# Query and key projections of a hybrid attention block: one wide matmul for the high and low activations, with the PSUM banks of attention moved

## The chip, the cores and the metric

The kernel runs on one core of one Trainium2 chip. The metric is the device time of one execution, in microseconds. Only that one core works; no other core's clock or traffic plays a part. TensorE (matmuls into PSUM), VectorE, ScalarE, GpSimd and the DMA queues each run their own stream of instructions and meet at semaphores.

## What is computed

One layer of an encoder block on 256 tokens of width 2048, all in float32, then a final normalisation. Cut to what matters here:

```python
h = rms_norm(x, norm_mix)
proj = h @ w_in                       # 2048 -> qa 1024, ka 256, va 256, qf 1024, kf 1024, vf 1024, f 16
qa, ka = rope(qa), rope(ka)           # group A: 16 query heads, 4 key heads, head width 64
out_a = swa_sink_attention(qa, ka, va, sinks)          # sliding window of two 64-token chunks
log_f = log_sigmoid(f_logit + b_f)
out_b = forgetting_attention(qf, kf, vf, log_f)        # group B ("FoX"): 16 heads, causal, no rotary
x = x + concat([out_a, out_b]) @ w_o
h = rms_norm(x, norm_ffn)
x = x + conv_gated_ffn(h, w_up, conv_w, conv_b, w_down)   # d_ff 5632
return rms_norm(x, norm_final)
```

## The kernel before

**Float32 products from split parts.** Every operand of a projection is split into a high part that TensorE's replicated float32 type (R32) holds exactly, and a low part, the rest. ScalarE makes the high part (`split_hi`, L417: `hi` from `raw`), VectorE the low part (`split_lo`, L645: `lo` = `raw` - `hi`). A product is then high times high, high times low and low times high: `mm3` (L960 to L964), three matmuls. The activations are held turned, features on partitions, in `act_split[:, 2, 16, 256]`: the high parts of the 16 blocks of 128 features (`act_hi`) beside their low parts (`act_lo`).

**Tiles of weights.** The weights stream through four slots (`RING`). A tile is 512 KB: 512 rows by 256 columns for `w_in` and `w_up`. Tiles are numbered through the kernel: 0 to 3 hold the values of group A and the gates, 4 to 7 the keys of group A, 8 + 16 j + s is step s of quad j (j from 0 to 3), from 72 on come W_o, the up and the down projection. For tile t SyncE loads `raw` when `lo_done` shows tile t - 4 split, ScalarE splits when `mm_done` shows tile t - 4 multiplied, then VectorE, then TensorE multiplies (`pe.wait_ge(lo_done, t + 1)`). Both splitters run three tiles ahead (`LEAD`): at step s of a quad they split the tile of step s + 3.

**Quads.** A quad is four query heads of each group and takes 16 tiles, four each for qa, kf, qf (function `features`, weights stationary, the result features by tokens) and vf (function `tokens`, activations stationary). In `features` a pair (c, b) is one block of 128 input features by one block of 128 output features: three matmuls of 256 columns. The results of qa and qf went to bank `acc[0]`, kf, vf and the keys of group A to `acc[1]`: both blocks b of one result share one bank of 512 columns.

**Out of PSUM.** VectorE scales kf (step 8) and qf (step 12) out of PSUM in one instruction each (L773), and makes the rotary embedding: `rope` (L675, from PSUM times cosine, step 5) and `rope_rest` (L680, L682, step 9), where `swap` is a copy with the halves of each head exchanged, made by ScalarE's `rope_swap` (L435, step 4) out of PSUM in four instructions.

**Attention** of quad j - 1 runs beside the projections of quad j. The steps are constants: scores behind step 13, the maxima and biases at 14 (VectorE reads the FoX scores at L735, ScalarE takes exponentials), then in the next quad the turned copies through `tr_ps` at steps 1 to 3 (ScalarE L506, L510), the products with the values behind step 4 (L1070 `values_a` into `pv_ps`, L1081 `values_fox` into `acc[2]`), and their evacuation at 5 (ScalarE L514, VectorE L765).

**Around the keys of group A** (tiles 4 to 7), ScalarE's stream is: high part of tile 10, `rope_swap`, `fcum`, wait for `krope_s`, four copies to `kta` (L484), high part of tile 11 and on. VectorE's: low part of tile 10, rope in three instructions, low part of tile 11 and on. GpSimd waits for `kta`, copies group A's operands, writes `nft` to memory, reads it back as `key_bias` four times 512 KB, and adds the causal mask to it in eight instructions (L394, L395), in quad 0.

**The up projection** (`up_step`, L1206 to L1213) multiplies otherwise: one matmul of the high weights with `act_split[:, :, k, :]`, 512 columns, high and low activations side by side in one bank, and one of the low weights with the high activations, 256 columns, onto the first half. ScalarE and VectorE add the two halves of the bank when they take it out.

## Time and profile before

| what | value |
|---|---|
| median of 3 runs | 1089.55 us (1089.06 to 1089.94) |
| the profiled execution's own time | 1088.71 us |
| its span, first to last instruction | 1086.8 us |
| TensorE busy | 1075.6 us, 99% of the span |
| VectorE / ScalarE / GpSimd busy | 710.2 / 579.6 / 27.4 us |
| HBM read and written | 199.06 and 2.11 MB |

The profile is of one execution. Engine names in its rows: PE is TensorE (PEld its weight loads), DVE is VectorE, ACT ScalarE, POOL GpSimd, SP SyncE; a q behind a name is that engine's sequencer. Matmuls overlap in the pipeline, so a matmul's listed duration is longer than its share of TensorE's time. Idle time stands in brackets in a timeline row with what ended it. The time lies 1.9 us over the span, for what comes before the first and after the last instruction.

### The profile page before, as it was taken

Reading aid. Unit: us, or ns where it says so; the run is one execution under the profiler, and the core shown is the slowest. Engines: PE = TensorE matmul, PEld = TensorE weight load, DVE = VectorE, ACT = ScalarE, POOL = GpSimd, SP = SyncE. Lnnn points to the kernel's source line nnn. Section 1 sums busy time; section 2 is a strip of 40 time slices with the busy share of each in tenths; the row PEclk is TensorE's granted clock in tenths of the full one; section 3 lists DMA queues with packets and bytes.
Section 4 is the critical chain, followed back from the end, with each engine's and each line's share of the span. In section 5 each row is a group of like instructions: output and inputs, shape, how many; then the busy total and the mean of one; then the engine's idle time right before and its main releaser. Section 6 shows DMA issues by size and latency. Waiting matters only on the chain.

```text
span 1086.8 us, 18571 instructions
## 1 busy us (share of the span) xinstructions
PE 1075.6 (99%) x6553; PEld 947.1 (87%) x6553; DVE 710.2 (65%) x1023; ACT 579.6 (53%) x890; POOL 27.4 (3%) x42
## 2 busy tenths in 40 slices
PE   8999999999999999999999999999999999999997
PEld 8999999998888888888888888888888888888885
DVE  5667575656555787777777777877777444454543
ACT  6847373736455655565555555566555434343432
POOL 1150000000000000000000000000000000000000
PEclk9999999999999999999999999999999999999999
DMA  9685645454555666656665566656666656656662
GB/s 275 192 268 152 174 138 174 143 179 142 174 174 176 179 202 191 183 172 208 190 196 177 180 206 192 183 169 209 193 192 212 206 187 190 192 184 189 191 190 101
DMA packets 169796, 201.69 MB, mean 186 GB/s; under 512 B 8580, under 2 KB 136292, under 8 KB 169632
## 3 DMA queue, kind: packets, MB, share of 16 engines
q1 hardware_dynamic: 168464, 197.49, 58.9%
q0 software_dynamic: 976, 3.37, 1.0%
q8 instruction: 24, 0.39, 0.1%
q10 hardware_dynamic: 320, 0.34, 0.1%
q14 instruction: 12, 0.10, 0.0%
HBM read 199.06 MB, written 2.11 MB: 185 GB/s over the span
## 4 chain that ended last, share of the span: by engine, by line
PE 98%; DMA 1%; SPq 0%; DVE 0%; ACT 0%; issue 0%; DVEq 0%
PE tr_ps L1210 15%; PE acc L1210 15%; PE acc L962 8%; PE acc L963 8%; PE acc L964 8%; PE acc L1212 8%; PE tr_ps L1212 8%; PE sc_ps L962 5%; PE sc_ps L963 5%; PE sc_ps L964 5%; PE tr_ps L963 4%; PE tr_ps L962 4%; PE tr_ps L964 4%; DMA nat<-x 1%; PE tr_ps L1098 0%; PE acc L1081 0%
## 5 line engine op out<-in xcount | busy, mean ns | idle before, releaser
L645 DVE TENSOR_TENSOR lo<-raw,hi 128x1024 fp32r<-128x1024 f32 (+1 forms) x368 | 448.5, 1230 | 285.7 <-ACT hi L417 285.4
L417 ACT ACTIVATE hi<-raw 128x1024 fp32r<-128x1024 f32 (+1 forms) x368 | 384.6, 1058 | 262.1 <-PE sc_ps L964 78.9
L1210 PE MATMUL tr_ps<-act_split,hi 128*128 128x512 f32 x704 | 245.3, 391 | 0.0
L1210 PE MATMUL acc<-act_split,hi 128*128 128x512 f32 x704 | 245.0, 391 | 0.0
L1212 PE MATMUL acc<-act_split,lo 128*128 128x256 f32 x704 | 197.1, 280 | 0.0
L1212 PE MATMUL tr_ps<-act_split,lo 128*128 128x256 f32 x704 | 197.1, 280 | 0.0
L1210 PEld LDWEIGHTS acc<-act_split,hi 128*128 128x128 f32 x704 | 131.6, 187 | 28.9
L1210 PEld LDWEIGHTS tr_ps<-act_split,hi 128*128 128x128 f32 x704 | 131.7, 187 | 28.8
L1212 PEld LDWEIGHTS tr_ps<-act_split,lo 128*128 128x128 f32 x704 | 133.0, 189 | 0.1
L1212 PEld LDWEIGHTS acc<-act_split,lo 128*128 128x128 f32 x704 | 133.1, 189 | 0.0
L962 PE MATMUL acc<-act_split,hi 128*128 128x256 f32 x416 | 118.9, 286 | 0.0
L964 PE MATMUL acc<-act_split,lo 128*128 128x256 f32 x416 | 117.7, 283 | 0.0
L963 PE MATMUL acc<-act_split,hi 128*128 128x256 f32 x416 | 117.7, 283 | 0.0
L962 PEld LDWEIGHTS acc<-act_split,hi 128*128 128x128 f32 x416 | 79.7, 192 | 0.5 <-issue 0.5
L963 PEld LDWEIGHTS acc<-act_split,hi 128*128 128x128 f32 x416 | 79.8, 192 | 0.0
L964 PEld LDWEIGHTS acc<-act_split,lo 128*128 128x128 f32 x416 | 79.7, 192 | 0.0
L964 PE MATMUL sc_ps<-hi,g_lo 128*128 128x512 f32 x176 | 69.4, 395 | 0.0
L963 PE MATMUL tr_ps<-lo,g_hi 128*128 128x512 f32 x176 | 69.4, 395 | 0.0
L962 PE MATMUL tr_ps<-hi,g_hi 128*128 128x512 f32 x176 | 69.4, 395 | 0.0
L962 PE MATMUL sc_ps<-hi,g_hi 128*128 128x512 f32 x176 | 69.4, 394 | 0.0
L963 PE MATMUL sc_ps<-lo,g_hi 128*128 128x512 f32 x176 | 69.4, 394 | 0.0
L964 PE MATMUL tr_ps<-hi,g_lo 128*128 128x512 f32 x176 | 69.4, 394 | 0.0
(207 smaller groups left out, 1292.3 us busy)
## 6 DMA issues: line engine op xcount, KB each, us to landing
raw<-w_up SPq DMA_DIRECT2D x176, 512.0 KB, 4.4
raw<-w_down SPq DMA_DIRECT2D x88, 512.0 KB, 4.5
raw<-w_in SPq DMA_DIRECT2D x72, 512.0 KB, 3.7
raw<-w_o SPq DMA_DIRECT2D x32, 512.0 KB, 3.8
nat<-x SPq DMA_DIRECT2D x8, 256.0 KB, 6.3
key_bias<-nft_dram POOLq DMA_DIRECT2D x4, 512.0 KB, 8.3
result<-nat SPq DMA_DIRECT2D x7, 256.0 KB, 3.0
gfin<-norm_final POOLq DMA_DIRECT2D x1, 1024.0 KB, 7.9
```

The source lines that it names most:

```text
L417: act.activation(hi[:, slot, 0:n], raw[:, slot, 0:n], ACT.Copy).then_inc(hi_done, 1)
L645: dve.tensor_tensor(lo[:, slot, 0:n], raw[:, slot, 0:n], hi[:, slot, 0:n].bitcast(F32), ALU.subtract).then_inc(lo_done, 1)
L962: pe.matmul(dst, a_hi, b_hi, start=start, stop=False, skip_group_check=True)
L963: pe.matmul(dst, a_hi, b_lo, start=False, stop=False, skip_group_check=True)
L964: return pe.matmul(dst, a_lo, b_hi, start=False, stop=True, skip_group_check=True)
L1210: pe.matmul(up_banks[v][b].rearrange("p (a n) -> p a n", a=2), wh[:, c, b * P:(b + 1) * P], act_split[:, :, k, :], start=k == 0, stop=Fals ...
L1212: ins = pe.matmul(up_banks[v][b][:, 0:S], wl[:, c, b * P:(b + 1) * P], act_hi[:, k], start=False, stop=True, skip_group_check=True)
```

## The change

`features` takes up the form of the up projection: for each pair (c, b) one matmul of the high weights with high and low activations side by side (512 columns) and one of the low weights with the high activations (256 columns). One result now fills two banks, so the five banks `acc[0..2]`, `pv_ps` become one tensor `pj` of four: qa and qf in banks 0 and 1 (pair 0), the keys of group A and kf in 2 and 3 (pair 1), vf in 2. The products with the values and the cumulated gates go to `tr_ps`, the second pair of FoX scores to `pj[:, 3]` and `pj[:, 0]`.

To add the halves, ScalarE copies the second half of both banks into the result's place in SBUF (`cross_half`), and VectorE adds the first half from PSUM (`join_halves`); then kf and qf are scaled in place, and rope runs on `rope_a` in SBUF. `rope_swap` now reads `rope_a`, so it waits for `join_halves`: at step 6 in a quad (was 4), and VectorE's three rope instructions stand together at step 7 (were at 5 and 9). TensorE's waits: the first tile of a quad also waits for `read_s` (VectorE has read the previous quad's FoX scores), `values_a` for all three turned copies, and the scores for `kq_s` (kf and qf scaled). The diff's core:

```diff
-QUAD_STEPS = 7
+QUAD_STEPS = 8
...
-        acc = [ps(f"acc{i}", [P, 512]) for i in range(3)]
+        pj = ps("pj", [P, 4, 512])
         sc_ps = ps("sc_ps", [P, 2, 512])
         tr_ps = ps("tr_ps", [P, 2, 512])
-        pv_ps = ps("pv_ps", [P, 512])
-        x_banks = [acc[0][:], acc[2][:], acc[1][:], sc_ps[:, 0], sc_ps[:, 1], tr_ps[:, 0], tr_ps[:, 1], pv_ps[:]]
-
-        wo_banks = [(sc_ps[:, 0], sc_ps[:, 1]), (acc[0][:], acc[1][:])]
-        yt_banks = (acc[2][:], pv_ps[:])
-
-
-        fox_banks = [(tr_ps[:, 0], tr_ps[:, 1]), (acc[2][:], pv_ps[:])]
-
-        up_banks = [[tr_ps[:, 0], tr_ps[:, 1]], [acc[1][:], acc[2][:]]]
+        x_banks = [pj[:, 0], pj[:, 1], pj[:, 2], sc_ps[:, 0], sc_ps[:, 1], tr_ps[:, 0], tr_ps[:, 1], pj[:, 3]]
+
+        wo_banks = [(sc_ps[:, 0], sc_ps[:, 1]), (pj[:, 1], pj[:, 2])]
+        yt_banks = (pj[:, 3], pj[:, 0])
+
+
+        fox_banks = [(tr_ps[:, 0], tr_ps[:, 1]), (pj[:, 3], pj[:, 0])]
+
+        up_banks = [[tr_ps[:, 0], tr_ps[:, 1]], [pj[:, 0], pj[:, 1]]]
...
-            def rope_swap(bank, scale):
-
+            def rope_swap(scale):
+
+                part = rope_a[:].rearrange("p a n -> p (a n)")
                 for o in range(0, P, 32):
                     i = o ^ 32
-                    ins = act.activation(swap[o:o + 32].rearrange("p a n -> p (a n)"), bank[i:i + 32, :], ACT.Copy, scale=scale)
+                    ins = act.activation(swap[o:o + 32].rearrange("p a n -> p (a n)"), part[i:i + 32], ACT.Copy, scale=scale)
                 ins.then_inc(swap_s, 1)
+
+            def cross_half(pair, dst):
+
+                act.activation(dst[:], pj[:, 2 * pair:2 * pair + 2, S:2 * S], ACT.Copy).then_inc(half_s, 1)
...
                 if s == 3:
                     act.wait_ge(mm_done, T_KA + 4)
-                    rope_swap(acc[1], 1.0)
+                    cross_half(1, rope_a)
                     act.wait_ge(fcum_ps, 1)
-                    act.activation(fcum[:].rearrange("p a n -> p (a n)"), pv_ps[:, 0:MT * NH], ACT.Copy,
+                    act.activation(fcum[:].rearrange("p a n -> p (a n)"), tr_ps[:, 0, 0:MT * NH], ACT.Copy,
                                    scale=-1.0).then_inc(fcum_s, 1)
+                    act.wait_ge(evac_d, 1)
+                    rope_swap(1.0)
                     act.wait_ge(krope_s, 1)
...
                 for s in range(QUAD_TILES):
+                    if s in (8, 12):
+                        act.wait_ge(mm_done, j * QUAD_TILES + (T_QUAD + s))
+                        if attend:
+                            act.wait_ge(sf_s, j * 2)
+                        if s == 8:
+                            cross_half(1, kf)
+                        else:
+                            cross_half(0, qf)
                     split_hi(j * QUAD_TILES + (T_QUAD + s + LEAD), (s + LEAD) % RING)
                     if s == 4:
                         act.wait_ge(mm_done, j * QUAD_TILES + (T_QUAD + 4))
                         act.wait_ge(krope_s, j + 1)
-                        rope_swap(acc[0], QSCALE)
+                        cross_half(0, rope_a)
+                    if s == 6:
+                        act.wait_ge(evac_d, j * 3 + 2)
+                        rope_swap(QSCALE)
...
-            def rope(bank, scale, tmp):
-
-                dve.scalar_tensor_tensor(tmp[:], bank[:].rearrange("p (a n) -> p a n", a=2), scale,
-                                         cos_r[:].unsqueeze(1).broadcast_to([P, 2, S]), ALU.mult, ALU.mult).then_inc(evac_d, 1)
-
-            def rope_rest(dst, tmp):
-
+            def join_halves(pair, dst, n):
+
+                dve.wait_ge(half_s, n)
+                dve.tensor_tensor(dst[:], dst[:], pj[:, 2 * pair:2 * pair + 2, 0:S], ALU.add).then_inc(evac_d, 1)
+                dve.wait_ge(evac_d, n)
+
+            def rope(dst, scale):
+
+                st.done(dve.scalar_tensor_tensor(rope_a[:], rope_a[:], scale,
+                                                 cos_r[:].unsqueeze(1).broadcast_to([P, 2, S]), ALU.mult, ALU.mult))
                 st.done(dve.tensor_tensor(swap[:], swap[:], sin_r[:].unsqueeze(1).broadcast_to([P, 2, S]), ALU.mult))
                 st.wait()
-                return dve.tensor_tensor(dst[:], tmp[:], swap[:], ALU.add)
+                return dve.tensor_tensor(dst[:], rope_a[:], swap[:], ALU.add)
...
-                    dve.wait_ge(mm_done, T_KA + 4)
+                    join_halves(1, rope_a, 1)
                     dve.wait_ge(swap_s, 1)
-                    rope(acc[1], 1.0, rope_a)
-                    dve.wait_ge(evac_d, 1)
-                    rope_rest(rope_b, rope_a).then_inc(krope_s, 1)
+                    rope(rope_b, 1.0).then_inc(krope_s, 1)
...
                 for s in range(QUAD_TILES):
                     if s in (8, 12):
-                        dve.wait_ge(mm_done, j * QUAD_TILES + (T_QUAD + s))
-                        bank, dst, scale = (acc[1], kf, 1.0) if s == 8 else (acc[0], qf, QSCALE)
-                        dve.scalar_tensor_tensor(dst[:], bank[:].rearrange("p (a n) -> p a n", a=2), scale,
-                                                 r1b[:].unsqueeze(1).broadcast_to([P, 2, S]), ALU.mult,
-                                                 ALU.mult).then_inc(evac_d, 1)
+                        pair, dst, scale = (1, kf, 1.0) if s == 8 else (0, qf, QSCALE)
+                        join_halves(pair, dst, j * 3 + (3 if s == 8 else 4))
+                        dve.scalar_tensor_tensor(dst[:], dst[:], scale, r1b[:].unsqueeze(1).broadcast_to([P, 2, S]), ALU.mult,
+                                                 ALU.mult).then_inc(kq_s, 1)
                     split_lo(j * QUAD_TILES + (T_QUAD + s + LEAD), (s + LEAD) % RING)
-                    if s == 5:
-                        dve.wait_ge(mm_done, j * QUAD_TILES + (T_QUAD + 4))
+                    if s == 4:
+                        join_halves(0, rope_a, j * 3 + 2)
+                    if s == 7:
                         dve.wait_ge(swap_s, j + 2)
-                        rope(acc[0], QSCALE, rope_a)
-                    if s == 9:
-                        dve.wait_ge(evac_d, j * 3 + 2)
-                        rope_rest(qa, rope_a).then_inc(krope_s, 1)
+                        rope(qa, QSCALE).then_inc(krope_s, 1)
...
-            def features(t, slot, bank, kt, a_hi, a_lo, first):
+            def features(t, slot, pair, kt, first):
 
                 pe.wait_ge(lo_done, t + 1)
                 wh, wl = narrow(hi, slot), narrow(lo, slot)
                 for c in range(4):
+                    k = 4 * kt + c
                     for b in range(2):
-                        ins = mm3(bank[:, b * S:(b + 1) * S], wh[:, c, b * P:(b + 1) * P], wl[:, c, b * P:(b + 1) * P],
-                                  a_hi[:, 4 * kt + c], a_lo[:, 4 * kt + c], start=first and c == 0 and b == 0)
+                        bank = pj[:, 2 * pair + b]
+                        pe.matmul(bank.rearrange("p (a n) -> p a n", a=2), wh[:, c, b * P:(b + 1) * P], act_split[:, :, k, :],
+                                  start=first and c == 0, stop=False, skip_group_check=True)
+                        ins = pe.matmul(bank[:, 0:S], wl[:, c, b * P:(b + 1) * P], act_hi[:, k], start=False, stop=True,
+                                        skip_group_check=True)
                 ins.then_inc(mm_done, 1)
...
                 pe.wait_ge(evac_d, j * 3 + 4)
+                pe.wait_ge(kq_s, j * 2 + 2)
...
-                pe.wait_ge(pt_s, q * 3 + 1)
+                pe.wait_ge(pt_s, q * 3 + 3)
                 for v, c0, c1, moving in ((0, 0, 2, lambda h: turned_a[:, h, :, :, 0:64]),
                                           (1, 2, 3, lambda h: turned_a[:, h, 1:2, :, 64:128]),
                                           (2, 3, 4, lambda h: turned_a[:, h, 0:1, :, 64:128])):
                     for h in range(2):
-                        dst = pv_ps[h * HD:(h + 1) * HD].rearrange("k (e c n) -> k c e n", e=2, c=4)[:, c0:c1]
+                        dst = tr_ps[h * HD:(h + 1) * HD, 0].rearrange("k (e c n) -> k c e n", e=2, c=4)[:, c0:c1]
                         ins = pe.matmul(dst, vq[:, v], moving(h), start=v == 0, stop=True, skip_group_check=True)
...
             def values_fox(q):
 
-                pe.wait_ge(pt_s, q * 3 + 3)
                 pe.wait_ge(evac_a, q + 2)
                 for p in range(2):
                     for k in range(2):
                         for h in range(2):
                             i = p * 2 + h
-                            ins = pe.matmul(acc[2][h * HD:(h + 1) * HD, p * S + k * P:(p + 1) * S], vf[:, k, i * HD:(i + 1) * HD],
+                            ins = pe.matmul(tr_ps[h * HD:(h + 1) * HD, 1, p * S + k * P:(p + 1) * S], vf[:, k, i * HD:(i + 1) * HD],
...
                                 pe.wait_ge(evac_d, j * 3 + 1)
+                                pe.wait_ge(read_s, j * 2)
                             else:
                                 pe.wait_ge(evac_a, 1)
                         if n == 1:
                             if attend:
                                 pe.wait_ge(evac_a, j + 1)
                             else:
-                                pe.wait_ge(swap_s, 1)
                                 pe.wait_ge(evac_d, 1)
                         if n == 2:
-                            pe.wait_ge(swap_s, j + 2)
                             pe.wait_ge(evac_d, j * 3 + 2)
                         if n == 3:
                             pe.wait_ge(evac_d, j * 3 + 3)
                     t = j * QUAD_TILES + (T_QUAD + s)
                     if n < 3:
-                        features(t, kt, acc[n % 2], kt, act_hi, act_lo, kt == 0)
+                        features(t, kt, n % 2, kt, kt == 0)
                     else:
-                        tokens(t, kt, acc[1], kt, kt == 0, lambda: scores_ready(j, attend))
+                        tokens(t, kt, pj[:, 2], kt, kt == 0, lambda: scores_ready(j, attend))
...
```

The rest renames banks in the same way.

## Rows read from the trace of the kernel before

**Rows 1.** The page: TensorE's busy time, its granted clock in tenths, the chain by engine.
```profile
PE 1075.6 (99%) x6553; PEld 947.1 (87%) x6553; DVE 710.2 (65%) x1023; ACT 579.6 (53%) x890; POOL 27.4 (3%) x42
...
PEclk9999999999999999999999999999999999999999
...
PE 98%; DMA 1%; SPq 0%; DVE 0%; ACT 0%; issue 0%; DVEq 0%
```

**Rows 2.** Windows, one quad's length: window, length, busy PE, PEld, DVE, ACT, POOL.
```profile
107.02:160.26 53.24, 53.24 (x497) 51.91 (x497) 33.82 (x47) 29.58 (x61) 0.95 (x4) 1.00 0.55 158
```

**Rows 3.** Timeline (start, duration), TensorE in features tiles: first and last of 117.
```profile
107.77 0.28 PE L962 MATMUL acc<-act_split,hi 128*128 128x256 f32 x1
...
121.69 0.28 PE L964 MATMUL acc<-act_split,lo 128*128 128x256 f32 x1
```

**Rows 4.** Chain in order of time, up projection: first pair and the 34th.
```profile
400.26 0.23 PE tr_ps L1210
...
411.70 0.23 PE acc L1210
```

**Rows 5.** Timeline, 128x512 out of PSUM: a ScalarE copy, a VectorE instruction.
```profile
107.16 0.60 ACT L514 ACTIVATE mix_hi<-pv_ps 128x512 f32 x1
...
108.91 0.68 DVE L765 TENSOR_TENSOR mix_lo<-pv_ps,mix_hi 128x512 f32 x1
```

**Rows 6.** Timeline, end of quad 1: VectorE's last reading, TensorE's next quad.
```profile
140.43 0.47 DVE L735 SCALAR_TENSOR_TENSOR prob<-pv_ps,fq,key_bias 128x256 f32<-128x256 f32 x1
...
141.24 0.28 PE L962 MATMUL acc<-act_split,hi 128*128 128x256 f32 x1
```

**Rows 7.** Timeline: the last turned copy and the first product with the values.
```profile
155.12 0.81 ACT L510 ACTIVATE prob_t<-tr_ps 128x768 f32<-128x768 f32 x1 [1.76 <-PE tr_ps L1098]
...
157.87 1.09 PE L1070 MATMUL pv_ps<-prob_t,prob 128*64 128x256 f32 x12
```

**Rows 8.** Timeline, ScalarE behind the keys of group A.
```profile
37.71 2.39 ACT L435 ACTIVATE swap<-acc 32x512 f32<-32x512 f32 x4 [0.24 <-PE acc L964]
...
42.38 2.60 ACT L484 ACTIVATE kta<-rope_b 64x512 f32<-64x512 f32 x4 [2.06 <-DVE rope_b L682]
45.00 2.01 ACT L417 ACTIVATE hi<-raw 128x1024 fp32r<-128x1024 f32 x2
```

**Rows 9.** Timeline, VectorE there: low part of tile 10, then of 11 to 14.
```profile
38.21 1.23 DVE L645 TENSOR_TENSOR lo<-raw,hi 128x1024 fp32r<-128x1024 f32 x1
...
46.10 4.86 DVE L645 TENSOR_TENSOR lo<-raw,hi 128x1024 fp32r<-128x1024 f32 x4 [3.75 <-ACT hi L417]
```

**Rows 10.** Timeline, TensorE: first matmul of tile 11 and of tile 19.
```profile
48.05 0.28 PE L962 MATMUL acc<-act_split,hi 128*128 128x256 f32 x1
...
71.09 0.28 PE L962 MATMUL acc<-act_split,hi 128*128 128x256 f32 x1
```

**Rows 11.** Timeline, VectorE beside GpSimd's mask additions: kf, tile 19's split, rope.
```profile
62.69 0.68 DVE L773 SCALAR_TENSOR_TENSOR kf<-acc,r1b 128x512 f32<-128x512 f32 x1
65.35 2.16 DVE L645 TENSOR_TENSOR lo<-raw,hi 128x1024 fp32r<-128x1024 f32 x1 [1.99 <-ACT hi L417]
...
69.68 1.77 DVE L680 TENSOR_TENSOR swap<-swap,sin_r 128x512 f32<-128x512 f32 x1
```

**Rows 12.** Timeline, GpSimd's mask additions: four of the eight.
```profile
58.45 1.97 POOL L394 TENSOR_TENSOR key_bias<-key_bias,mask_b 128x512 f32<-128x512 f32 x1 [3.90 <-DMA key_bias<-nft_dram]
...
63.89 1.29 POOL L395 TENSOR_TENSOR key_bias<-key_bias,mask_b 128x512 f32<-128x512 f32 x1
...
68.63 2.28 POOL L394 TENSOR_TENSOR key_bias<-key_bias,mask_b 128x512 f32<-128x512 f32 x1
70.87 1.74 POOL L395 TENSOR_TENSOR key_bias<-key_bias,mask_b 128x512 f32<-128x512 f32 x1
```

**Rows 13.** Timeline, ScalarE: the high part of tile 19.
```profile
64.26 1.06 ACT L417 ACTIVATE hi<-raw 128x1024 fp32r<-128x1024 f32 x1 [3.37 <-DMA raw<-w_in]
```

**Rows 14.** Timeline, TensorE: the longest idle time, at the beginning.
```profile
10.20 0.44 PE L948 MATMUL acc<-ident,nat 128*128 128x128 f32 x2 [1.74 <-DMA nat<-x]
```

More of the change, by code:

```diff
@@ L460, in _ @@
                     act.wait_ge(mm_done, 4)
-                    for m, bank in enumerate((acc[0], acc[2])):
-                        ins = act.activation(va[:, 2 * m], bank[:, 0:256], ACT.Copy, scale=r1c[:, m:m + 1])
+                    for m in range(MT):
+                        ins = act.activation(va[:, 2 * m], pj[:, m, 0:256], ACT.Copy, scale=r1c[:, m:m + 1])
                     ins.then_inc(evac_a, 1)
@@ L688, in _ @@
                     dve.wait_ge(evac_a, 1)
-                    for m, bank in enumerate((acc[0], acc[2])):
-                        st.done(dve.scalar_tensor_tensor(fg[:, 0, m], bank[:, 256:VA_COLS], r1c[:, m:m + 1],
+                    for m in range(MT):
+                        st.done(dve.scalar_tensor_tensor(fg[:, 0, m], pj[:, m, 256:VA_COLS], r1c[:, m:m + 1],
                                                          bf_b[:], ALU.mult, ALU.add))
@@ L996, in _ @@
                     pe.wait_ge(xlo, k + 1 if k else 4)
-                    for m, bank in enumerate((acc[0], acc[2])):
-                        ins = mm3(bank[:, 0:VA_COLS], act_hi[:, k, m * P:(m + 1) * P],
+                    for m in range(MT):
+                        ins = mm3(pj[:, m, 0:VA_COLS], act_hi[:, k, m * P:(m + 1) * P],
                                   act_lo[:, k, m * P:(m + 1) * P], wh[:, c], wl[:, c], start=k == 0)
@@ L1220, in up_step @@
                             pe.wait_ge(diag2_s, m + 1)
-                            ins = pe.matmul(acc[0][:, m * P:(m + 1) * P], ones[:], diag2[:, m], start=True, stop=True)
+                            ins = pe.matmul(pj[:, 2, m * P:(m + 1) * P], ones[:], diag2[:, m], start=True, stop=True)
                         ins.then_inc(r2_ps, 1)
```

26 lines of the change are left out of this document (13 added, 13 removed).

## The prediction

> **What bounds the kernel now.** I read the page first: TensorE is busy 99% of the span, 98% of the chain that ended last is its work, and its granted clock is full, 2.4 GHz, in every slice [rows 1]. Then the stages: in a whole quad of attention and projections TensorE has no idle time at all (53.24 of 53.24 us) while VectorE works 33.8 us and ScalarE 29.6 us [rows 2]. So the time is the number of matmuls by their pitch, plus whatever makes TensorE wait. A matmul's listed duration (0.28 us) overlaps its neighbours; what counts is the distance from start to start. In a features tile of before, 116 such distances fill 107.77 to 121.69 us: 120.0 ns each, so 360 ns for the three products of one (c, b) [rows 3]. The up projection already uses the form that the change brings in: one 512-column and one 256-column matmul for each pair. There 33 pairs fill 400.26 to 411.70: 346.7 ns a pair [rows 4].
>
> **Fewer matmuls.** There are 52 features tiles: 4 for the keys of group A and 12 in each of 4 quads. Each has 8 pairs, so 416 triples become 416 pairs: 416 x (360.0 - 346.7) = 5.5 us less, 0.107 us in each tile, all on the path. Nothing is removed from the tokens tiles, W_o, up or down.
>
> The Trainium skill speaks against this much: "TensorE: Matmul & The Clock Gate", section "Wait — 56ns, not 53.3ns?", gives a fixed cost of about 2.5 ns for each warm matmul beyond its columns, so merging two into one would save 2.5 ns, or 416 x 2.5 = 1.0 us in all (an estimate from that page). Here the trace disagrees, 13.3 ns a pair between two stages of this same kernel, and the measurement is used in the sum.
>
> **Extra work off the path.** Each of the three features results of a quad now costs a ScalarE copy of a half out of PSUM (128x512, 0.60 us) and a VectorE addition (0.68 us) [rows 5]. The second scaling instruction (kf, qf, rope) stays, but reads SBUF in place of PSUM. That is 1.8 us of ScalarE and 2.0 us of VectorE per quad on engines that have 23 and 19 us idle [rows 2]. Hidden as totals; the question is what is late where TensorE waits.
>
> **Waits that are moved, quads 1 to 3.** (a) The next quad's first tile now waits for VectorE's last reading of the second pair of FoX scores, since both use bank pj[:, 0]. That reading starts at 140.43, takes 0.47 and ends at 140.90; TensorE's first matmul of the next quad starts at 141.24 [rows 6]. Both are measured from the end of tile 13 of the quad, through stretches that the change leaves alone, so 0.34 us of margin remain: cost 0, at most 0.2 us a quad for the waking. (b) values_a now waits for the last turned copy, which ends at 155.93; its first matmul starts at 157.87 [rows 7], and the tile between gets 0.1 us shorter: cost 0. (c) kf and qf are ready 0.60 + 0.68 + 0.69, about 2.0 us after their last matmul, where scores wait for qf only at the end of the second tile after it, over 5 us later: cost 0. If that cover went, each us would be paid once a quad.
>
> **First late tile: tile 11.** After the keys of group A (tiles 4 to 7), ScalarE makes four swapped copies (37.71 to 40.10), waits 2.06 us for VectorE's rope, makes kta (42.38 to 44.98) and only then splits tile 11 (from 45.00) [rows 8]. VectorE's part of that split runs 46.10 to 47.33 [rows 9], and TensorE starts tile 11 at 48.05 [rows 10]: 0.7 us of margin. After the change the chain is longer. ScalarE copies the half at about 37.5, VectorE adds at the end of its queued split (38.21 + 1.23 = 39.4) until 40.1, and only now can ScalarE start the swaps, just when it was done with them before. So everything behind shifts by the four swaps: 2.39 us as from PSUM, at most the 2.60 of the four copies from SBUF in kta [rows 8]. I take 2.5, as they read SBUF but are no wider. Tile 11's low part is ready at 49.85; TensorE, 7 tiles x 0.107 sooner, is there at 47.3. Stall: 2.5 us (2.4 to 2.7). Queued behind these instructions are the later splits of both engines (12 to 15) and nft: all shift, but tile 12 is needed 2.8 us after tile 11 and is split 1.2 us after it, so only the first is late.
>
> **Second late tile: tile 19.** In quad 0 GpSimd adds the mask to key_bias in eight instructions from 58.45 to 72.6. In that time VectorE's two-source instructions from SBUF alternate with GpSimd's: a split took 2.16 us instead of 1.23, rope's 128x512 multiplication 1.77 where that shape takes 0.68 elsewhere [rows 5, 9], while kf, which read PSUM, took 0.68 right in it [rows 11]. GpSimd's own, 1.29 alone, went to 2.28 beside the multiplication [rows 12]. So each waits for the other's current instruction. Before, VectorE had little to do there and waited for tile 19's weights (ScalarE got them at 64.26 after an idle time of 3.37 us [rows 13]); its low part was ready at 67.51 [rows 11], 3.6 us before TensorE's 71.09 [rows 10]. The change puts five instructions ahead of that split: rope's three, moved from steps 5 and 9 to step 7, and kf's addition and scaling. With the 2.5 us shift GpSimd starts at 60.95. VectorE: split of tile 18 waits until 63.5, ends 64.7; three rope instructions at 1.29 + 0.6 each, to 70.4; addition, reading PSUM, to 71.0; kf scaling to 72.2; GpSimd's next to 73.5; split of tile 19 ends at 74.7. TensorE is there at 49.85 + 8 x 2.774 = 72.0. Stall: 2.6 us. The unshown price is that of SCALAR_TENSOR_TENSOR with both inputs in SBUF beside GpSimd. The nearest rows are 0.68 (same operation, one input in PSUM, not held up) and 1.77 (another operation, both in SBUF, held up) [rows 11]. With the first for both such instructions, the split ends at 70.9 and there is no stall. I take the second, since what differs between those rows is where the inputs lie.
>
> The Trainium skill's page "SBUF — State Buffer", section "Who interferes with whom", says it so: a VectorE instruction with two SBUF inputs contends with a GpSimd instruction that reads SBUF. By that rule the stall comes, as in my sum; that it holds for this operation no row here shows.
>
> Tile 20's split would then end at 77.1 against 77.4 on TensorE: barely in time.
>
> **Sum.** -5.5 + 2.5 + 2.6 = -0.4 us on the profiled execution's 1088.71 (span 1086.8 and 1.9 around it): 1088.3. The median of the runs, 1089.55, lies 0.84 higher, so 1089.1.
>
> **Rivals.**
> 1. Only the first stall: scalar_tensor_tensor is not held up by GpSimd, or GpSimd's work lies elsewhere. 1089.55 - 5.5 + 2.5 = 1086.5. For it: kf's 0.68. Against: the split and the multiplication of [rows 11].
> 2. Neither stall: 1084.0. It needs tile 11's chain to shift by under 0 us (0.7 of margin, less the 0.75 gained); the order of the instructions excludes that nearly.
> 3. Slower by the clock. The longest idle of TensorE in the trace is 1.74 us, before 10.20, and the clock stayed full through it [rows 1, 14]; both stalls are longer than that. If the clock falls to 1.2 GHz after one, matmuls take twice as long: one tile's 2.77 us at the low level costs as much again. 1089.1 + 2.8 = 1091.9. It decides from an idle time somewhere above 1.74 us.
> 4. The change does not do what it says: a 512-column matmul costs here what two of 256 columns cost, since the features operands come in another order than up's. Then nothing is gained and the stalls stay: 1089.55 + 5.1 = 1094.6. Against it: rows 3 and 4 have the same shapes, types and stationary width. By the 2.5 ns of the Trainium skill's "TensorE: Matmul & The Clock Gate" it would be 1.0 less.
>
> **Chances.** Both stalls 0.52 (own range 1088.3 to 1090.3), first only 0.25, neither 0.05, clock 0.15, no gain 0.03. A difference under 0.2% (2.2 us) can't be told from none. Faster than 1087.4: rivals 1 and 2 and a little of the forecast, 0.32. Within: 0.50. Slower than 1091.7: 0.18. The range for 8 in 10 goes from rival 1 with its stall 0.6 short, 1085.8, to rival 3, 1092.0.
>
> **What the changed profile would show.** Pairs at 346.7 ns in the features stage; one idle of TensorE of about 2.5 us at 47 us that ends with VectorE's split of tile 11; one of about 2.6 us at 72 us that ends with the split of tile 19, with rope's instructions at 1.9 us each ahead of it; none at the quads' beginnings; a quad of about 52.0 us from quad 1 on; W_o, up and down unchanged. The prediction is wrong if rope's instructions run in 0.69 us beside GpSimd, if the features pitch isn't that of up, if the granted clock shows a dip, or if a wait for the read scores appears.

## The result, and the profile after

The changed kernel took 1093.18 us (median of 20 runs, 1088.44 to 1095.33) against 1089.33 us for the kernel before on the same chip (20 runs, 1088.67 to 1090.7): ratio 1.0029, 95% interval 1.0021 to 1.0037. It is slower by 0.3%, and 1093.18 lies above the range of the prediction, 1085.8 to 1092.0. The profiled execution took 1093.45 us with a span of 1091.6, so 4.8 us more span than before.

The page of the changed kernel, the same lines as [rows 1] (busy time of each engine, the granted clock in tenths, the chain by engine), shows little:

```profile
PE 1077.7 (99%) x6137; PEld 928.8 (85%) x6137; DVE 719.3 (66%) x1036; ACT 587.2 (54%) x903; POOL 27.1 (2%) x42
...
PEclk9999999999999999999999999999999999999999
...
PE 95%; DVE 2%; ACT 2%; DMA 1%; issue 0%; SPq 0%; DVEq 0%; ACTq 0%
```

There are 416 matmuls fewer, yet TensorE is busy 2.1 us longer (matmuls at a low clock, below). VectorE and ScalarE have come into the chain. The page's clock row still reads 9 everywhere: its slices are 27 us wide and hide what follows.

The waits of TensorE (line waited for, us in total, times, longest):

```profile
PE pj L989 <- DVE lo L662: 4.1, 2, 2.1
```

Two waits of TensorE for a low part; nothing like it stands in the kernel before. They are at tile 11 and tile 19 (timeline, TensorE, last matmul before and first one behind each wait; it answers to [rows 10]):

```profile
48.00 0.28 PE L991 MATMUL pj<-act_split,lo 128*128 128x256 f32 x1
50.32 0.50 PE L989 MATMUL pj<-act_split,hi 128*128 128x512 f32 x1 [2.04 <-DVE lo L662]
...
74.45 0.28 PE L991 MATMUL pj<-act_split,lo 128*128 128x256 f32 x1
76.81 0.50 PE L989 MATMUL pj<-act_split,hi 128*128 128x512 f32 x1 [2.09 <-DVE lo L662]
```

From start to start 2.32 and 2.36 us, where a matmul of 256 columns has 0.12: 2.2 and 2.2 us lost. What the prediction had only as a rival stands in narrow windows around them (window, length, busy PE, PEld, DVE, ACT, POOL; then the granted clock):

```profile
48.00:50.00 2.00, 0.28 (x2) 0.00 (x0) 0.96 (x1) 2.00 (x3) 1.68 (x4) 1.00 0.00 0
50.00:51.00 1.00, 0.68 (x3) 0.64 (x4) 1.00 (x2) 1.00 (x3) 0.80 (x2) 0.90 0.00 0
51.00:54.00 3.00, 3.00 (x11) 2.51 (x11) 2.81 (x4) 2.94 (x4) 0.03 (x1) 0.50 0.76 222
...
72.00:76.00 4.00, 2.72 (x16) 2.12 (x14) 3.96 (x4) 2.11 (x2) 3.67 (x3) 1.00 0.01 3
76.00:80.00 4.00, 3.19 (x13) 2.77 (x14) 4.00 (x4) 0.00 (x0) 0.00 (x0) 0.76 0.45 134
80.00:84.00 4.00, 4.00 (x28) 3.80 (x28) 2.24 (x4) 1.55 (x2) 0.00 (x0) 0.81 0.96 304
```

Behind each wait the clock is at half (1.2 GHz) for some 3.4 us, and half of that is lost: (1 - 0.90) x 1 + (1 - 0.50) x 3 + (1 - 0.95) x 2 = 1.7 us for the first (the last term is the window 54 to 56), 0.24 x 4 + 0.19 x 4 = 1.7 us for the second.

**The pitch.** In this kernel the distance of two pairs is 346.5 ns in some stretches and 353.4 in others, with the same code and shapes (timeline, TensorE; 28 distances in the first two rows, 50 in the last two):

```profile
220.14 0.40 PE L989 MATMUL pj<-act_split,hi 128*128 128x512 f32 x1
...
229.84 0.40 PE L989 MATMUL pj<-act_split,hi 128*128 128x512 f32 x1
```
```profile
56.54 0.40 PE L989 MATMUL pj<-act_split,hi 128*128 128x512 f32 x1
...
74.21 0.40 PE L989 MATMUL pj<-act_split,hi 128*128 128x512 f32 x1
```

9.70 / 28 = 346.4 ns and 17.67 / 50 = 353.4 ns. Within the features tiles, without the low clock and what stands between them, the mean is 351.0, so the gain against 360 is 416 x 9.0 = 3.7 us.

**The account of the profiled executions:** -3.7 (fewer matmuls) + 2.2 + 2.2 (waits) + 1.7 + 1.7 (half clock) + 0.5 (the second wait for rows of x) = +4.6 us, where the spans differ by 4.8. The last term is the start of this row, 10.74, against 10.20 in [rows 14]:

```profile
10.74 0.66 PE L963 MATMUL pj<-ident,nat 128*128 128x128 f32 x4 [0.41 <-DMA nat<-x]
```

No part of the change touches it. It is still there at the first features matmul, 25.56 in the kernel before and 26.13 here (timeline, TensorE); behind the last one both kernels take the same time.

```profile
25.56 0.28 PE L962 MATMUL acc<-act_split,hi 128*128 128x256 f32 x1
```
```profile
26.13 0.39 PE L989 MATMUL pj<-act_split,hi 128*128 128x512 f32 x1
```

**The other executions.** The mean granted clock of an execution tells how much of it ran at half clock; one fall of 3.4 us lowers it by 0.0016. Of the 20 executions, 2 are at 0.998, as is the profile of before, and took 1088.44 and 1089.82 us. The 9 at 0.996 and 0.997 took 1090.9 to 1093.99, the 7 at 0.995 took 1093.1 to 1094.41, the 2 at 0.994 took 1095.16 and 1095.33. So the kernel's time goes with the falls of its clock, and without them it is about that of the kernel before.

### The profile page after: what moved, and what is told of

Same layout as the page of the kernel before. It is cut to its first block, busy times and chain, and to the rows that moved or that the text cites. A ratio compares the mean times of both kernels' runs of the same rounds, so it can differ in the third digit from the quotient of the medians.

```text
span 1091.6 us, 17780 instructions
## 1 busy us (share of the span) xinstructions
PE 1077.7 (99%) x6137; PEld 928.8 (85%) x6137; DVE 719.3 (66%) x1036; ACT 587.2 (54%) x903; POOL 27.1 (2%) x42
## 4 chain that ended last, share of the span: by engine, by line
PE 95%; DVE 2%; ACT 2%; DMA 1%; issue 0%; SPq 0%; DVEq 0%; ACTq 0%
PE tr_ps L1228 15%; PE pj L1228 15%; PE pj L1230 8%; PE tr_ps L1230 8%; PE pj L989 7%; PE sc_ps L977 5%; PE sc_ps L979 5%; PE sc_ps L978 5%; PE tr_ps L978 4%; PE tr_ps L979 4%; PE tr_ps L977 4%; PE pj L991 4%; PE pj L977 3%; PE pj L978 3%; PE pj L979 3%; DVE lo L662 1%
## 5 line engine op out<-in xcount | busy, mean ns | idle before, releaser
L1228 PE MATMUL pj<-act_split,hi 128*128 128x512 f32 x704 | 245.0, 391 | 0.0
L1230 PE MATMUL pj<-act_split,lo 128*128 128x256 f32 x704 | 197.1, 280 | 0.0
L1228 PEld LDWEIGHTS pj<-act_split,hi 128*128 128x128 f32 x704 | 131.6, 187 | 28.9
L989 PE MATMUL pj<-act_split,hi 128*128 128x512 f32 x416 | 151.1, 405 | 4.1 <-DVE lo L662 4.1
L1230 PEld LDWEIGHTS pj<-act_split,lo 128*128 128x128 f32 x704 | 133.1, 189 | 0.0
L991 PE MATMUL pj<-act_split,lo 128*128 128x256 f32 x416 | 117.8, 283 | 0.0
L989 PEld LDWEIGHTS pj<-act_split,hi 128*128 128x128 f32 x416 | 79.4, 191 | 23.6 <-DVE lo L662 4.8
L991 PEld LDWEIGHTS pj<-act_split,lo 128*128 128x128 f32 x416 | 79.9, 192 | 0.0
L606 ACT ACTIVATE conv_o<-ub,cst 128x256 f32<-128x256 f32 x88 | 48.3, 596 | 22.2 <-DVE ub L865 22.2
L977 PE MATMUL pj<-hi,act_split 128*128 128x256 f32 (+1 forms) x160 | 46.1, 288 | 0.0
```

The source lines that it names most:

```text
L606: act.activation(conv_o[:, v, b], ub[:, v, b, 2:S + 2], ACT.Identity, scale=tap(2, i * 2 + (b + v * FB)), bias=tap(3, i * 2 + (b + v * FB) ...
L977: pe.matmul(dst, a_hi, b_hi, start=start, stop=False, skip_group_check=True)
L989: pe.matmul(bank.rearrange("p (a n) -> p a n", a=2), wh[:, c, b * P:(b + 1) * P], act_split[:, :, k, :], start=first and c == 0, stop=Fals ...
L991: ins = pe.matmul(bank[:, 0:S], wl[:, c, b * P:(b + 1) * P], act_hi[:, k], start=False, stop=True, skip_group_check=True)
L1228: pe.matmul(up_banks[v][b].rearrange("p (a n) -> p a n", a=2), wh[:, c, b * P:(b + 1) * P], act_split[:, :, k, :], start=k == 0, stop=Fals ...
L1230: ins = pe.matmul(up_banks[v][b][:, 0:S], wl[:, c, b * P:(b + 1) * P], act_hi[:, k], start=False, stop=True, skip_group_check=True)
```

## The experiments

**The theory** after the result: two waits, each with a fall of the clock behind it, and a gain of 3.7. The wait at tile 11 comes from ScalarE's swapped copies, which now wait for VectorE's addition; that at tile 19 from VectorE instructions with both inputs in SBUF that GpSimd's masks hold up. The ratio of each experiment is against executions of the kernel before beside it, with medians of 1088.97 (experiments 1 to 3 and 6), 1089.85 (4, 7, 8 and the first kernel of 5) and 1089.11 us (9 and the second of 5). **Rivals:** that the two waits are one cause (a shift of everything); that tile 19 is late through its weights and not through GpSimd; that the fall of the clock is no result of the waits; that the 512-column form gains nothing.

**1. Tile 11 split earlier.** Both splitters take tile 11 before the rotary work on the keys.

```diff
+                    split_hi(T_QUAD + LEAD, LEAD)
                     act.wait_ge(evac_d, 1)
                     rope_swap(1.0)
...
                     join_halves(1, rope_a, 1)
+                    split_lo(T_QUAD + LEAD, LEAD)
                     dve.wait_ge(swap_s, 1)
```

> The changed kernel, with tile 11 split before ScalarE's four swaps (VectorE's part right behind the first addition of halves). Theory (two stalls and a fall of the clock behind each): the idle time of 2.2 us before tile 11 and the half-speed stretch at 50.5 to 54.5 us go, some 4 us; TensorE reaches tile 19 about 4 us sooner but GpSimd and rope only 1 us sooner, so the second stall grows by about 3 us. Time 1092 to 1093, hardly less than the changed kernel's 1093.2. Rival (a stall is paid once and for itself): 1089, with the second stall as it was.

Measured 1095.1 us (1093.01 to 1095.67), ratio 1.0054 (1.004 to 1.0068): above the 1092 to 1093 expected, and no faster than the changed kernel. The first wait is gone and the second has grown (waits; VectorE's timeline; windows):

```profile
PE pj L993 <- DVE lo L664: 4.4, 1, 4.4
```
```profile
67.71 1.77 DVE L700 SCALAR_TENSOR_TENSOR rope_a<-rope_a,cos_r 128x512 f32<-128x512 f32 x1
69.41 1.78 DVE L702 TENSOR_TENSOR swap<-swap,sin_r 128x512 f32<-128x512 f32 x1
71.22 1.64 DVE L704 TENSOR_TENSOR qa<-rope_a,swap 128x512 f32<-128x512 f32 x1
```
```profile
72.00:76.00 4.00, 0.63 (x2) 0.53 (x3) 3.97 (x5) 0.57 (x1) 0.31 (x1) 0.66 0.00 0
76.00:80.00 4.00, 4.00 (x14) 3.42 (x13) 2.72 (x3) 0.00 (x0) 0.00 (x0) 0.50 0.81 241
```

TensorE is ready for tile 19 some 3.8 us sooner (70.8 against 74.6), but VectorE's chain stands where it stood: rope starts at 67.71 here and at 67.66 in the changed kernel. GpSimd's masks and the arrival of tile 18's weights set it here (ScalarE's split of them starts at 65.20, behind `[2.38 <-DMA raw<-w_in]`), not TensorE. What was saved ahead is lost again there: one wait of 4.4 us for two of 2.2, and one long stretch of low clock that costs 2.4 us behind the wait's end at 75.37, for two of 1.7. So the two waits have two causes, and curing the first alone gained nothing. That it made the kernel slower isn't shown: the profiled execution took 1093.01 us, against 1093.45 of the changed kernel. A second one at the same mean clock of 0.995 took 1093.55, where the changed kernel's 7 took 1093.1 to 1094.41, and the three at 0.994 (1095.1 to 1095.67) are near the changed kernel's two (1095.16 and 1095.33). Why there are more of these isn't known; no profile caught one.

**2. The masks left out.** GpSimd's eight additions to `key_bias` become four memsets, which write only; the causal mask is left out of the computation.

```diff
-                pool.tensor_tensor(kb[:, :, 0:P], kb[:, :, P:2 * P], mask, ALU.add)
-                pool.tensor_tensor(kb[:, :, 2 * P:384], kb[:, :, 2 * P:384], mask, ALU.add).then_inc(bias_s, 1)
+                pool.memset(kb[:, :, 0:P], 0.0).then_inc(bias_s, 1)
```

> The changed kernel with GpSimd's eight mask additions replaced by four memsets that only write, so the causal mask and the addition are left out. Theory: rope's three instructions and kf's scaling take 0.69 us each instead of 1.1 to 1.8, the idle time before tile 19 goes with the fall of the clock behind it: 1093.2 - 2.0 - 2.0, about 1089. If scalar_tensor_tensor is slow for its operands in SBUF and not because of GpSimd, the instructions stay at 1.7 and the time at 1093.

Measured 1088.83 us (1087.52 to 1090.71), ratio 0.9998 (0.9989 to 1.0007), as expected. Rope as it ran in the changed kernel, then here (timeline, VectorE):

```profile
67.66 1.78 DVE L698 SCALAR_TENSOR_TENSOR rope_a<-rope_a,cos_r 128x512 f32<-128x512 f32 x1
69.36 1.78 DVE L700 TENSOR_TENSOR swap<-swap,sin_r 128x512 f32<-128x512 f32 x1
71.17 1.67 DVE L702 TENSOR_TENSOR qa<-rope_a,swap 128x512 f32<-128x512 f32 x1
72.76 0.68 DVE L693 TENSOR_TENSOR kf<-kf,pj 128x512 f32<-128x512 f32 x1
```
```profile
66.47 0.69 DVE L697 SCALAR_TENSOR_TENSOR rope_a<-rope_a,cos_r 128x512 f32<-128x512 f32 x1
67.07 0.68 DVE L699 TENSOR_TENSOR swap<-swap,sin_r 128x512 f32<-128x512 f32 x1
67.79 0.69 DVE L701 TENSOR_TENSOR qa<-rope_a,swap 128x512 f32<-128x512 f32 x1
68.39 0.68 DVE L692 TENSOR_TENSOR kf<-kf,pj 128x512 f32<-128x512 f32 x1
```

Only the instructions with both inputs in SBUF change, from 1.7 to 0.69 us; kf's addition, which reads PSUM, takes 0.68 in both. The second wait is gone, the first stays at 2.1 us with one fall of the clock behind it. So the late tile 19 is GpSimd's doing and no matter of its weights.

**3 and 4. The waits filled with matmuls.** In the changed kernel TensorE multiplies `ones` ahead of tiles 11 and 19; the results are not used. First 18 and 20 of them, then half as many.

```diff
                     t = j * QUAD_TILES + (T_QUAD + s)
+                    if not attend and s in (3, 11):
+                        warm(18 if s == 3 else 20)
```

> The changed kernel with 18 and 20 filler matmuls of 128 columns, whose result nobody reads, ahead of tiles 11 and 19: TensorE works through most of both stalls and no tile is ready sooner. Theory (the price beyond the stalls is the clock): it stays at 2.4 GHz and about 4 us go, 1089 to 1089.5, although work was added. Rival (the excess over my forecast has another cause): 1093 or slightly more.

> The changed kernel with 9 and 10 filler matmuls ahead of tiles 11 and 19, 2.0 and 2.2 us by the 0.11 us that each half of one took in e3_filler, where they filled 3.9 and 4.4 us, more than the stalls. Theory (the clock is the excess): the same stalls, filled, clock at 2.4 GHz: 1089.0 - 3.7 + 4.6 = 1089.9. Rival: the clock is no cost of its own, 1093.

Measured 1093.69 us for the first (1093.59 to 1096.38; ratio 1.0048, 1.0034 to 1.0062) and 1091.96 us for the second (1090.05 to 1094.83; 1.0023, 1.0014 to 1.0031). Both miss their number, and the first miss is a plain mistake in their size: each filler became two matmuls of 0.11 us, so that TensorE was held 3.9 us at tile 11 and 4.4 us at tile 19, where it had waited 2.2 (the first kernel: timeline, TensorE, and windows):

```profile
48.54 4.18 PE L949 MATMUL tr_ps<-ones 128*128 128x128 f32 x36
52.47 0.48 PE L989 MATMUL pj<-act_split,hi 128*128 128x512 f32 x1
```
```profile
48.00:52.00 4.00, 4.00 (x37) 3.91 (x36) 2.38 (x3) 3.98 (x7) 2.52 (x5) 1.00 0.02 3
52.00:56.00 4.00, 4.00 (x27) 3.58 (x26) 2.61 (x3) 2.79 (x4) 1.13 (x2) 1.00 0.93 276
```

Even so they settle what they were for: the clock stays at 1.00 through both places in both kernels. The first one's time is then a sum without any term for the clock: 1089.0 - 3.7 + 3.9 + 4.4 = 1093.6, against 1093.69 measured. In the second, TensorE is held from 48.80 to 50.99 and from 73.71 to 75.86, which is as long as the waits were. The second one's profiled execution took 1091.28 us with no wait for a low part, 2.2 us less than that of the changed kernel; -3.4 was expected from the clock. Two things that have nothing to do with the fillers take 1.3 us of it back. The first features matmul starts 0.7 us later (26.82 against 26.13), and the 12 features tiles of the last quad run at 353 ns a pair where the changed kernel's run at 347 (96 pairs, 0.6 us; timeline, TensorE, 28 distances):

```profile
26.82 0.39 PE L989 MATMUL pj<-act_split,hi 128*128 128x512 f32 x1
...
216.92 0.39 PE L989 MATMUL pj<-act_split,hi 128*128 128x512 f32 x1
...
226.80 0.40 PE L989 MATMUL pj<-act_split,hi 128*128 128x512 f32 x1
```

The median gained 1.2 us (0.6 by the ratios, since the kernel before beside it had a median of 1089.85). The executions lie from 1090.05 to 1094.83 us. The fall behind x, below, can be only a part of that, since those at a mean clock of 0.998 and 0.999 go up to 1092.67. The level of the pitch is a candidate, 416 x 6.9 = 2.9 us between all pairs at one and at the other, but no run shows it for an execution that wasn't profiled.

**5. The same wait put into the kernel before.** Four more ScalarE copies (3.2 us) ahead of tile 11's high part, in one kernel, and two (1.6 us) in another; nothing else of the change is in them.

```diff
                                            ACT.Copy).then_inc(kta_s, 1)
+                    act.activation(conv_o[:].rearrange("p a b n -> p (a b n)"), nat[:, 0, 0:1024], ACT.Copy)
+                    act.activation(silu[:].rearrange("p a n -> p (a n)"), nat[:, 0, 0:512], ACT.Copy)
...
```

> The kernel of before with four ScalarE copies that nobody reads, 3.2 us in all, ahead of the high part of tile 11: with its 0.7 us of margin TensorE waits 2.5 us there, and nothing of the change is in it. Theory: the idle time and a fall of the clock to 1.2 GHz behind it, worth 1.7 us: 1089.0 + 2.5 + 1.7 = 1093.2. Rival (an idle time costs itself alone): 1091.5.

> The kernel before, with two more ScalarE copies (128x1024 and 128x512, 1.6 us together) ahead of its high part of tile 11; the kernel before has 0.7 us of margin there, so TensorE should wait about 0.9 us before tile 11. If the clock falls only behind a longer wait (the one of the run with four copies was 2.1 us), it stays full and the time is the kernel before plus 0.9: about 1090.3. If any wait of this place lets it fall, about 1.7 us more: 1092.

Measured 1093.12 us (1091.06 to 1094.88), ratio 1.0028 (1.0016 to 1.004), for four copies and 1091.55 us (1089.69 to 1093.86), ratio 1.0018 (1.0007 to 1.0029), for two. The waits came out at 2.1 and 0.6 us (waits of the two kernels):

```profile
PE acc L966 <- DVE lo L649: 2.1, 1, 2.1
```
```profile
PE acc L964 <- DVE lo L647: 0.6, 1, 0.6
```

Behind the 2.1 us the clock fell (0.88 from 48 to 52, 0.69 from 52 to 56), behind the 0.6 it did not. The executions of the first kernel fall into two groups: 1091.06 to 1091.56 us at a mean granted clock of 0.998 and 0.999, and 1092.7 to 1094.88 at 0.996 and 0.997. The lower group is the kernel before plus about the wait (1088.9 + 2.1 = 1091.0); the other is 1.4 to 3.6 us above the lower one's median of 1091.3. So by the mean clocks the fall comes in some executions and not in others.

The kernel with two copies shows why its median missed. Its profiled execution has a fall in quite another place (windows):

```profile
10.00:12.00 2.00, 0.39 (x2) 0.40 (x3) 0.68 (x1) 0.00 (x0) 0.00 (x0) 0.78 1.05 352
12.00:14.00 2.00, 2.00 (x11) 2.00 (x10) 0.37 (x1) 1.22 (x4) 0.00 (x0) 0.50 1.06 347
14.00:16.00 2.00, 2.00 (x17) 2.00 (x16) 1.57 (x5) 1.57 (x3) 0.00 (x0) 0.87 1.13 351
```

That is the wait for rows of x at the start, 1.74 us in the profile of before [rows 14] and 3.2 us here. It varies from one execution to the next, and where it is long the clock falls behind it as well: 0.22 x 2 + 0.50 x 2 + 0.13 x 2 = 1.7 us. The kernel before has this too. Its 21 executions beside the first experiments are 16 at a clock of 0.998 or 0.999 with a median of 1088.85 us, and 5 at 0.996 or 0.997 with one of 1090.79. The mean clock doesn't part the two everywhere: beside the later experiments some executions of the kernel before at 0.998 took up to 1090.25 us, and one at 0.997 took 1088.53. The four executions of the kernel with two copies at 0.998 and 0.999, 1089.69 to 1090.82 us, are about 1.2 us above that first group, near the 0.9 expected; the six others run from 1091.5 to 1093.86.

**6. Both causes moved.** Tile 11 early as in the first experiment, and the masks of quads 1 to 3 behind quad 0's rotary work.

```diff
                 pool.wait_ge(d_bias[n], 16)
+                if n == 1:
+                    pool.wait_ge(krope_s, 2)
```

> e1_tile11_early, and GpSimd adds the mask for quad 0 alone before rope, for the other quads only after quad 0's rope. Theory: neither stall nor fall of the clock; the pair's pitch is left: 1089.4 - 5.5 = 1083.9, up to 1085 if tile 19's weights land late. Rival (the 512-column form gains nothing in this stage, or the bank moves cost): 1089 or more.

Measured 1090.43 us (1088.19 to 1092.49), ratio 1.0009 (1.0 to 1.0018): over 5 us above the 1083.9 to 1085 expected. Rope ran in 0.69 us an instruction, but the masks then met the splits of tiles 19 to 22, which now took 8.96 us for four instead of 4.9 (timeline, ScalarE and VectorE; waits):

```profile
66.43 1.06 ACT L418 ACTIVATE hi<-raw 128x1024 fp32r<-128x1024 f32 x1 [2.35 <-DMA raw<-w_in]
```
```profile
72.58 8.96 DVE L666 TENSOR_TENSOR lo<-raw,hi 128x1024 fp32r<-128x1024 f32 x4
```
```profile
PE pj L995 <- DVE lo L666: 3.0, 1, 3.0
```

A fall of the clock stands behind the wait (0.57 from 76 to 78, 0.58 from 78 to 80), and in this execution one behind the 1.9 us wait for x as well. The first row shows a second hold: tile 18's weights land late, while GpSimd's queue reads back 2 MB of `key_bias`. That the one delays the other was argued, not isolated; in experiment 7, which reads back a quarter of it there, ScalarE doesn't wait for them. Moving the masks by some us within quad 0 only moves the place where they hold VectorE up.

**7. The masks quad by quad.** Tile 11 early, and GpSimd reads back and masks only the 512 KB of `key_bias` that the next scores need, once a quad.

```diff
+            bias_of(0)
+            for j in range(1, QUADS):
                 pool.wait_ge(mixlo_s, j * 2)
                 copy_group_a(j)
                 pool.tensor_copy(fq[:], fcum[:, :, bass.ds(j * 4, 4)]).then_inc(fq_s, 1)
+                bias_of(j)
```

> e1_tile11_early, and GpSimd reads back and masks key_bias for one quad at a time: quad 0's 512 KB at once, those of quads 1 to 3 after the products with the values in their own quad. So neither the 2 MB burst nor the eight additions stand beside quad 0's rope. Theory (nothing but the two stalls, the clock behind them and the burst stood against the gain): no idle of TensorE over 0.5 us, clock full, and the features pairs' pitch as measured in the changed kernel (351 ns against 360) is left: 1089.0 - 416 x 0.009 = 1085.3. Rival (the moved banks or the moved steps cost something in every quad): 1088 or more.

Measured 1085.81 us (1084.56 to 1085.98), ratio 0.9958 (0.9946 to 0.9971): faster than both kernels. TensorE waits for no split, and its clock is 1.00 in every window from 44 to 80 us. VectorE at the place where rope had taken 5.2 us (timeline):

```profile
65.09 0.68 DVE L703 SCALAR_TENSOR_TENSOR rope_a<-rope_a,cos_r 128x512 f32<-128x512 f32 x1
65.70 0.68 DVE L705 TENSOR_TENSOR swap<-swap,sin_r 128x512 f32<-128x512 f32 x1
66.41 0.69 DVE L707 TENSOR_TENSOR qa<-rope_a,swap 128x512 f32<-128x512 f32 x1
```

The profiled span is 1084.0 us, 2.8 less than before, although the first features matmul starts 1.2 us later (26.78 against 25.56, behind the rows of x): 4.0 us are gained from there on.

```profile
26.78 0.39 PE L996 MATMUL pj<-act_split,hi 128*128 128x512 f32 x1
```

**8. The matmuls back to 256 columns**, in the kernel of experiment 7, so that only the form of the product differs.

```diff
-                        pe.matmul(bank.rearrange("p (a n) -> p a n", a=2), wh[:, c, b * P:(b + 1) * P], act_split[:, :, k, :],
-                                  start=first and c == 0, stop=False, skip_group_check=True)
+                        for a in range(2):
+                            pe.matmul(bank[:, a * S:(a + 1) * S], wh[:, c, b * P:(b + 1) * P], act_split[:, a, k, :],
+                                      start=first and c == 0 and a == 0, stop=False, skip_group_check=True)
```

> e5_bias_by_quad with each 512-column matmul of features cut into two of 256 columns onto the same bank, as before the change; all else as in e5. Theory: 120 ns for each of the three, so e5 + 3.7, 1089.0. If the 512-column form gives more (my 13.3 ns a pair), e5 + 5.5; if it gives 2.5 ns a pair, e5 + 1.0.

Measured 1089.84 us (1088.56 to 1091.2), ratio 0.9999 (0.999 to 1.0008): 4.0 us over experiment 7, as are the two profiled spans (1088.0 and 1084.0). That is the gain of the form by itself, near the 3.7 of the changed kernel's pitch, and not the 5.5 of the prediction. This kernel also has all else that the change adds (the copies, the additions, the moved waits) with neither the late tiles nor the wide matmul, and it costs nothing that can be told from the kernel before.

**9. Another order of the pairs**, in the kernel of experiment 7: both 512-column matmuls of a block c, then both of 256.

```diff
                     for b in range(2):
                         bank = pj[:, 2 * pair + b]
                         pe.matmul(bank.rearrange("p (a n) -> p a n", a=2), wh[:, c, b * P:(b + 1) * P], act_split[:, :, k, :],
                                   start=first and c == 0, stop=False, skip_group_check=True)
+                    for b in range(2):
+                        bank = pj[:, 2 * pair + b]
                         ins = pe.matmul(bank[:, 0:S], wl[:, c, b * P:(b + 1) * P], act_hi[:, k], start=False, stop=True,
                                         skip_group_check=True)
```

> The kernel with GpSimd's masks by quad, with the two 512-column matmuls of a block c first and then the two of 256 columns, in place of alternating them. If the 353 in place of 347 ns of a pair comes from the meeting of a narrow matmul and a wide one behind it (its weights are loaded beside only 256 columns), then half of these meetings are gone and the pitch of a pair falls by up to 6 ns, 416 x 6 = 2.5 us: 1083.5. If it comes from something else, the time stays at 1085.8; if the load of a narrow one's weights behind a narrow one is what is exposed, it rises by some us.

Measured 1084.67 us (1084.53 to 1084.79), ratio 0.9957 (0.9941 to 0.9974), the best of all. The pitch of two pairs is 697 ns in every stretch, where experiment 7's kernel has 693 or 706 by stretch and 699.9 in the mean. So the order removes the slower of the two levels and does not reach the faster: 208 x 3.0 ns = 0.6 us, a quarter of the 2.5 that was forecast for that case. In the profiled executions, 1.1 us apart, the rest is again x: the first features matmul starts 0.6 us earlier (26.19 against 26.78). Between the medians, of 4 and 5 executions, it can't be told from chance.

## Why the prediction was wrong

**The clock (rival 3) is the step that failed.** The prediction priced one fall, 2.8 us, took it for a case beside the sum with a chance of 0.15, and argued that the clock had stayed full through an idle of 1.74 us [rows 14]. That row is one execution: the same wait at the start was 3.2 us in that of experiment 5's kernel with two copies, with the clock at half behind it. And the sum itself held two waits, 2.5 and 2.6 us, both above anything that had been seen to be harmless. A fall behind each of them, 2 x 1.7 = 3.4 us, belonged in the sum: -0.4 + 3.4 = +3.0, or 1092.5 us, against 1093.18 measured. Each fall was smaller than priced (1.7 for 2.8) and there were two. In all, the sum missed by +3.4 for the clock, +1.8 for the pitch (-3.7 for -5.5) and -0.7 for the two waits (4.4 for 5.1): +4.5, where the medians miss by 4.1. The two executions whose mean clock shows no fall, 1088.44 and 1089.82 us, lie about the forecast of 1089.1. The filled waits of experiments 3 and 4 and the added wait of experiment 5 show that the fall hangs on the wait and on nothing else of the change.

**The pitch was mis-sized.** The form does gain, so rival 4 is out: experiment 8 puts it at 4.0 us. But rows 3 and 4 gave 5.5 by carrying up's 346.7 ns over to all 416 pairs; most features stretches run at 353. The stretch of up is constant in the kernel before and in the changed one, and that it had to be so in another stage was assumed.

**The first late tile: right.** 2.5 us forecast, 2.2 measured. ScalarE's swaps start at 40.61 behind `[1.78 <-DVE rope_a L693]` and take 2.56 us from SBUF, against 2.39 [rows 8]; tile 11's high part starts at 47.95, the low part at 49.04. Experiment 1 removes the wait by moving two instructions.

**The second late tile: right in its mechanism, with luck in its size.** 2.6 forecast, 2.2 measured, but both ends of it came later than forecast: rope started at 67.66 and not at 64.7, since tile 18's split stood at 65.45 and not at 63.5, and TensorE was there at 74.6 and not at 72.0, held up by the low clock behind the first wait, the later rows of x and the smaller gain. The two shifts nearly cancel. The unshown price, SCALAR_TENSOR_TENSOR with both inputs in SBUF beside GpSimd, was taken as 1.77 from the row of the multiplication [rows 11] and came out at 1.78; experiment 2 brings it to 0.69 by taking GpSimd's reads away. By the Trainium skill's "SBUF — State Buffer", section "Who interferes with whom", a VectorE instruction with two SBUF inputs contends with a GpSimd instruction that reads SBUF. The traces agree: 1.78 beside the mask additions, 0.69 beside the memsets, and 0.68 for the addition with an input in PSUM. Rivals 1 and 2 fall with it.

**The 2.5 ns of the Trainium skill.** "TensorE: Matmul & The Clock Gate", section "Wait — 56ns, not 53.3ns?", would give 1.0 us for the whole merging. The runs disagree: 4.0 us, or 9.6 ns for each matmul removed. Which part of a matmul's cost the page's figure leaves out is not shown by them.

**The waits that were moved, the extra copies and additions: right, at 0.** No wait of TensorE at the beginnings of quads, none for the read scores, none for `kq_s`; W_o, up and down are unchanged, and experiment 8 stands level with the kernel before.

**What the order of the causes did.** The prediction treated the two late tiles as a sum of independent terms. They are not: experiment 1 shows that TensorE, there 3.8 us sooner, waits 4.4 us for tile 19 where it had waited 2.2, since VectorE's chain is tied to GpSimd and the DMA queues (the tile was ready only 1.4 us sooner). In the changed kernel the first wait partly hides the second.

## What to carry to other kernels

A wait of TensorE of 2 us in a dense stream can cost more than its length: add the low clock behind it to the sum (1.7 us here, in most executions), and for the margin look at the clock of narrow windows in several executions, since a page of 27 us slices and one profile show neither. Before work is put ahead of a split on VectorE, look at what GpSimd reads in that stretch, for each VectorE instruction with both inputs in SBUF may then take much longer (1.7 to 1.8 for 0.69 us here). When two tiles are late, cure the later one first or both together: time won ahead of a tile whose due time is set elsewhere is only waited away.

## What the runs showed of the hardware

- **The clock behind a wait.** It fell to 1.2 GHz behind (in experiment 1 already in) waits of 2.0 us and more in every profile that has one (2.04 and 2.09 us in the changed kernel, 2.1, 2.1, 3.0, 3.2 and 4.4 in the experiments), stayed full behind 0.6, 1.5 and 1.74 us, and did the one and the other behind the 1.9 us wait for x in experiments 6 and 1. By the mean clocks it also stays full in some executions of the same kernels. Matmuls whose result nobody uses keep it up.
- **Two pitches for one stream.** Alternating matmuls of 512 and 256 columns run at 346.5 or 353.4 ns a pair. The slower level repeats every three pairs, 350, 361 and 349 ns. It changes only behind other work or a wait, is steady for tens of us, and differs between kernels with the same code in that place: the last quad ran at 347 ns in the changed kernel and in experiment 6's, and at 353 in experiments 1 to 4 and 7. What sets it is open; the order of experiment 9 has one level, 348.5.
- **Writes alone don't hold VectorE up.** GpSimd's memsets of 128x512 (0.53 us each) left VectorE's instructions at 0.69 us, where its additions of the same size made them 1.7.
